# Weight blocks split once and kept in DRAM, with the three token groups written out

## The reference

```
p = rms_norm(x, norm_g) @ w_in
aq, ak, av, ag, bq, bfg, bi, bg, ma, mb = split_projection(p)
...
ya = (attn_o * silu(ag)) @ w_ba
rn = rec_o * rsqrt(mean(rec_o * rec_o) + EPS) * g_norm
yb = (rn * silu(bg)) @ w_bb
merged = sigmoid(ma) * ya + sigmoid(mb) * yb
y = rms_norm(x + merged @ w_o, final_norm_gain)
```

## Time and profile before

| what | value |
|---|---|
| median of 3 runs | 1633.92 us (1633.89 to 1634.69) |
| the profiled execution's own time | 1631.52 us |
| its span in the profile | 1629.7 us |
| mean granted TensorE clock | 0.992 of full |
| PE busy | 1571.6 us, 96% |
| DVE busy | 896.3 us, 55% |
| ACT busy | 578.5 us, 35% |
| POOL busy | 437.2 us, 27% |
| moved by DMA | 124.35 MB, mean 76 GB/s |
| POOL L441, `w_lo` | 174 times, 423.0 us |
| ACT L473, `w_hi` | 174 times, 182.8 us |

### The profile page before, as it was taken

How to read it: one execution, slowest core, us unless ns; L and a number is a source line. 1 busy time by engine, 2 the same in 40 slices (tenths; PEclk the granted TensorE clock), 3 DMA queues, 4 the chain that set the end, 5 groups by cost and what they waited for, 6 DMA issues and landing times.

```text
span 1629.7 us, 24842 instructions
## 1 busy us (share of the span) xinstructions
PE 1571.6 (96%) x9679; PEld 1467.7 (90%) x9679; DVE 896.3 (55%) x1302; ACT 578.5 (35%) x1118; POOL 437.2 (27%) x186
## 2 busy tenths in 40 slices
PE   7999999999999899999999999999999999999997
PEld 5989899999997698989999999779898999999975
DVE  5667987721237356878782222745687868222213
ACT  5355443322123334555332212342455533222212
POOL 1321122332323232212223322423222222333320
PEclk9999999999999999999999999999999999999999
DMA  4211111122243321111112223433111111221231
GB/s 170 86 58 43 43 56 43 52 81 76 65 169 103 129 85 52 43 43 52 43 56 84 72 65 112 160 115 110 53 43 40 56 43 56 78 78 66 65 136 71
DMA packets 44856, 124.35 MB, mean 76 GB/s; under 512 B 6209, under 2 KB 17217, under 8 KB 44737
## 3 DMA queue, kind: packets, MB, share of 16 engines
q1 hardware_dynamic: 39408, 120.35, 23.2%
q10 hardware_dynamic: 5328, 2.37, 0.5%
HBM read 111.69 MB, written 11.01 MB: 75 GB/s over the span
## 4 chain that ended last, share of the span: by engine, by line
PE 87%; DVE 9%; issue 2%; ACT 1%; DMA 0%; DVEq 0%; ACTq 0%
PE bank L984 22%; PE bank L986 22%; PE bank L985 22%; PE bank L1185 4%; PE bank L1186 4%; PE bank L1187 4%; DVE rs L936 2%; PE bank L1156 1%; PE bank L1082 1%; PE bank L1138 1%; PE bank L1100 1%; PE bank L1114 1%; PE bank L1152 1%; PE bank L1124 1%; PE bank L1091 1%
## 5 line engine op out<-in xcount | busy, mean ns | idle before, releaser
L441 POOL TENSOR_TENSOR w_lo<-w_raw,w_hi 128x1024 fp32r<-128x1024 f32 x174 | 423.0, 2433 | 1152.5 <-ACT w_hi L473 1152.5
L984 PE MATMUL bank<-x_hi,w_hi 128*128 128x320 f32 (+1 forms) x2016 | 660.9, 328 | 10.1 <-issue 6.2
L986 PE MATMUL bank<-x_hi,w_lo 128*128 128x320 f32 (+1 forms) x2016 | 651.5, 323 | 0.0
L985 PE MATMUL bank<-x_lo,w_hi 128*128 128x320 f32 (+1 forms) x2016 | 651.1, 323 | 0.0
L984 PEld LDWEIGHTS bank<-x_hi,w_hi 128*128 128x128 f32 x2016 | 380.6, 189 | 19.0 <-issue 9.0
L985 PEld LDWEIGHTS bank<-x_lo,w_hi 128*128 128x128 f32 x2016 | 380.9, 189 | 0.1
L986 PEld LDWEIGHTS bank<-x_hi,w_lo 128*128 128x128 f32 x2016 | 380.3, 189 | 0.0
L473 ACT ACTIVATE w_hi<-w_raw 128x1024 fp32r<-128x1024 f32 x174 | 182.8, 1054 | 163.8 <-DMA w_raw<-in_w 157.2
L946 DVE TENSOR_TENSOR sig_a<-sig_a,bank 128x320 f32<-128x320 f32 (+1 forms) x48 | 25.0, 522 | 344.3 <-PE bank L986 344.3
L1185 PE MATMUL bank<-w_hi,m_hi 128*128 128x512 f32 (+1 forms) x288 | 116.2, 404 | 3.9 <-issue 3.7
L1187 PE MATMUL bank<-w_hi,m_lo 128*128 128x512 f32 (+1 forms) x288 | 113.9, 395 | 0.0
(11 more groups left out here) (169 smaller groups left out, 2034.8 us busy)
## 6 DMA issues: line engine op xcount, KB each, us to landing
w_raw<-in_w SPq DMA_DIRECT2D x174, 512.0 KB, 3.6
res<-in_x SPq DMA_DIRECT2D x15, 512.0 KB, 7.5
out_y<-res SPq DMA_DIRECT2D x15, 512.0 KB, 3.8
x_raw<-in_x_t SPq DMA_DIRECT2D x12, 384.0 KB, 7.1
x_raw<-in_x_t SPq DMA_DIRECT2D x12, 320.0 KB, 4.6
cos<-in_rope_cos SPq DMA_DIRECT2D x3, 352.0 KB, 3.8
sin<-in_rope_sin SPq DMA_DIRECT2D x3, 352.0 KB, 5.0
out_state_first<-s_first ACTq DMA_DIRECT2D x12, 64.0 KB, 3.3
```

Of the source, the lines that this page charges most:

```text
L441: pool.tensor_tensor(w_lo[s][:], w_raw[s][:], w_hi[s][:].bitcast(F32), ALU.subtract).then_inc(w_split, 1)
L984: pe.matmul(out, w_h, m_h, start=first, stop=False)
L985: pe.matmul(out, w_h, m_l, start=False, stop=False)
L986: return pe.matmul(out, w_l, m_h, start=False, stop=last_of_bank)
```

## The change

The weights are split only while the first group is worked on. High and low part of a slot are now one tile `w_both`; once a block is split, SP writes both parts (1 MB) to a DRAM tensor `w_parts`. In the later groups SP loads both parts from there straight into the slot, and TensorE waits for the load itself. ACT and POOL split nothing in these groups. In the first group the load of the next block into a slot also waits until the slot's parts are written (`w_kept`). The loop is gone: the three bodies stand in the program one behind the other.

```
     for s in range(SLOTS):
-        w_hi.append(own(f"w_hi{s}", [P, KT, P], F32R))
-        t, at, _ = sb(f"w_lo{s}", [P, KT, P], F32R)
-        w_lo.append(t)
-        w_raw.append(own(f"w_raw{s}", [P, KT, P], F32, at))
+        t, at, end = sb(f"w_both{s}", [P, 2, KT, P], F32R)
+        w_both.append(t)
+        w_hi.append(t[:, 0])
+        w_lo.append(t[:, 1])
+        w_raw.append(own(f"w_raw{s}", [P, KT, P], F32, (at + end) // 2))
+
+    parts = nc.dram_tensor("w_parts", (NB, P, 2, KT, P), F32).ap()
...
     def groups(eng, body):
 
-        with eng.Fori(0, GROUPS - 1) as g:
-            body(g, False)
-        body(GROUPS - 1, True)
+        for g in range(GROUPS):
+            body(g, g == GROUPS - 1)
...
                     wait_full(sp, gg, last, s, bank_of(last, s))
-            sp.dma_start(w_raw[SLOT[b]][:], w[b]).then_inc(w_landed[SLOT[b]], 16)
+                if gg == 0:
+                    sp.wait_ge(w_kept[SLOT[b]], 16 * (nth_in_slot(c) + 1))
+            if g == 0:
+                sp.dma_start(w_raw[SLOT[b]][:], w[b]).then_inc(w_landed[SLOT[b]], 16)
+            else:
+                sp.dma_start(w_both[SLOT[b]][:].bitcast(F32), parts[b]).then_inc(w_landed[SLOT[b]], 16)
+
+        def keep_block(b):
+
+            sp.wait_ge(w_split, b + 1)
+            sp.dma_start(parts[b], w_both[SLOT[b]][:].bitcast(F32)).then_inc(w_kept[SLOT[b]], 16)
...
+            kept = 0
             for b in range(SLOTS, NB):
+                while g == 0 and kept <= before(b)[0]:
+                    keep_block(kept)
+                    kept += 1
                 load_block(g, b, True, last)
...
+            if g == 0:
+                for b in range(kept, NB):
+                    keep_block(b)
             if not last:
                 for b in range(SLOTS):
                     load_block(g + 1, b, True)
...
             for b in range(FIRST, NB):
-                low(g, b)
+                if g == 0:
+                    low(g, b)
                 if b == NB - 5 and not last:
                     add_squares(pool, 1, g + 1)
-            if not last:
-                for b in range(FIRST):
-                    low(g + 1, b)
...
                 b = BLOCK[n] + 2
-                if b < NB:
-                    if b >= FIRST:
-                        high(g, b)
-                elif not last:
-                    high(g + 1, b - NB)
+                if g == 0 and FIRST <= b < NB:
+                    high(g, b)
...
+        def wait_block(g, b):
+
+            if g == 0:
+                pe.wait_ge(w_split, b + 1)
+            else:
+                pe.wait_ge(w_landed[SLOT[b]], 16 * (PER_SLOT[SLOT[b]] * g + nth_in_slot(b) + 1))
```

More of the change, by code:

```diff
@@ L205, in program @@
     res = own("res", [P, NT, D_MODEL], F32, at_ga_hi)
-    w_hi, w_lo, w_raw = [], [], []
+    w_both, w_hi, w_lo, w_raw = [], [], [], []
     for s in range(SLOTS):
-        w_hi.append(own(f"w_hi{s}", [P, KT, P], F32R))
-        t, at, _ = sb(f"w_lo{s}", [P, KT, P], F32R)
-        w_lo.append(t)
-        w_raw.append(own(f"w_raw{s}", [P, KT, P], F32, at))
+        t, at, end = sb(f"w_both{s}", [P, 2, KT, P], F32R)
[4 more added lines that the diff above has]
+    parts = nc.dram_tensor("w_parts", (NB, P, 2, KT, P), F32).ap()
     fgain = own("fgain", [P, D_MODEL])
@@ L272, in program @@
     w_high, w_split = sem("w_high"), sem("w_split")
+    w_kept = [sem(f"w_kept{s}") for s in range(SLOTS)]
     piece_used = sem("piece_used")
@@ L667, in body @@
                     ahead(f"wo{a}{s}")
-                    if (a, s) == (1, 3) and not last:
-                        high(g + 1, 2)
                 elif kind.startswith("x_"):
@@ L1021, in body @@
                     if s == 0:
-                        pe.wait_ge(w_split, NB * g + b + 1)
+                        wait_block(g, b)
                     wait_bank_free(pe, g, last, step, bank)
```

## The result

The changed kernel takes 1605.95 us (1605.1 to 1608.06, 4 runs) against 1634.31 us (1633.89 to 1635.53): a ratio of 0.9825, 95% interval 0.9811 to 0.984. It is 28.4 us faster; 21.7 had been forecast, and the time lies just under the range of 1606 to 1621. The profiled execution took 1606.46 us and its span is 1604.6 us. What follows is about the 6.7 us that the forecast lacked as much as about the 21.7.

What follows compares the result with a forecast made beforehand. PE's matmuls were taken to bound the kernel, leaving only its waits and low clock to win. Terms 6.9 + 9.8 + 4.1 + 0.5 + 0.4 = 21.7 us gave 1609.8 profiled, 1612.2 as median; range 1606 to 1621.

Steps and rivals of the forecast that it cites:

- gap at the first boundary: Loop's branch after group one: PE's stand falls from 5.71 to 0.49 us, 5.2 us won.
- clock behind it: PE's half-clock stretch after the 5.7 us issue wait at the loop's branch goes: 1.7 us won.
- `sc_t` waits: PE's waits for `sc_t` shrink in groups two and three as DVE's `sarg` and `f` run unstretched: 3.3 and 3.1 us.
- clock behind `sc_t` and `q_rot`: Half-clock stretches go: 2 x 1.7 us behind two `sc_t` waits, 1.7 behind the third group's `q_rot` wait.
- `q_rot` waits: `swap` in the chain drops from 2.1 to 0.89 us: 1.2 us of each wait in two groups, 2.4 us.
- `attn_o`: Third group's 0.54 us PE wait, put down to timing shifted behind a clock drop, goes: 0.5 us.
- state update and `sq_lo`: PE's `sq_lo` waits in two groups: 0.2 us won each, 0.4 in all; the read-out wait was not priced.
- issue gaps inside the groups: Small PE issue waits ahead of the output projections: given no term in the forecast, so 0 us.
- stores in group one: 58 stores of 1.05 MB on SP's queue: load and store take 6.1 to 6.6 us against 7.4 available; price zero.
- only the loop counts: Rival, chance 0.08: another engine takes over PE's waits at `sc_t` and `q_rot`; 6.9 us are left, 1627 us.
- PE is early and waits later: Rival, chance 0.08: PE reaches read-outs and `sq_lo` about 4 us earlier, giving half of 14.8 us back: 1619.6 us.
- The slower case: Rival, chance 0.06: stores hold loads back in group one, 9.2 us per block, 26 us of PE waits, 1638 us.

Runs made afterwards that it cites:

- ma0: Changed kernel, but one block, the 27th subtraction of a group, is loaded raw and split by ACT and POOL in every group: 1609.47 us.
- the loop alone: Kernel before with only the loop written out, every group still split by ACT and POOL: 1627.19 us against 1633.88, ratio 0.9958.
- the second store: Changed kernel, but each first-group block is stored twice, to two DRAM tensors, and the next load waits for both: 1669.7 us.

## Why the prediction was right and where it fell short

The terms of the sum, with what the two traces show for the second and third group and the boundaries:

| term | forecast | measured |
|---|---|---|
| gap at the first boundary | 5.2 | 5.4 (5.71 to 0.35) |
| clock behind it | 1.7 | 1.7 |
| `sc_t` waits | 6.4 | 7.0 (3.62 and 3.37, both to 0) |
| clock behind `sc_t` and `q_rot` | 5.1 | 5.1 (three drops) |
| `q_rot` waits | 2.4 | 2.7 (2.37 and 2.17 to 0.94 each) |
| `attn_o` | 0.5 | 0.5 (0.54 to 0) |
| state update and `sq_lo` | 0.4 | 4.1 (0.79 + 1.45 + 0.53 + 1.31, all to 0) |
| issue gaps inside the groups | 0 | 2.0 (3.7 to 1.9, and 0.49 to 0.26 at the second boundary) |
| stores in group one | 0 | 0 |
| sum | 21.7 | 28.5 |

The medians differ by 28.4. The profiled spans differ by 25.1 only; in the changed kernel's profiled execution the clock fell in the first group behind `q_rot` too and stayed low for 6.8 us behind `sc_t`, twice 1.7 us more than in that of before. That the sum meets the difference of the medians to 0.1 us is in part luck: the profiled execution of before lay 2.8 us under its median, that of the changed kernel 0.5 us over it.

**The mechanism was right.** The loop's branch, the stretched DVE operations and the clock behind the waits are where the time came from, each within 0.6 us, and the stores were free. In the long stretch of the first group a store landed in 6.5 us, which with the 0.4 us between the issues makes 6.9 us for load and store, where the prediction had 6.1 to 6.6; the loads are 7.4 us apart, so half a microsecond was to spare and not one. The Trainium skill ("DMA: Bandwidth & Descriptors", section "Measured (HBM→SBUF, 128 partitions, SWDGE, issued from GpSimd)") has 6.15 us for 1 MB. Here, on SP's queue, a load of 1 MB from `w_parts` took 4.8 us at its median from issue to landing, and a second store behind the first adds only 2 us. So the measurements decide against the sum of 9.2 us for load and store.

**The step that failed is the `sq_lo` term.** The prediction read the 0.23 us ahead of the operation at 818.28 as "waited only 0.23 us for DVE's own state update; beyond that it is bound to PE's projection". The timeline of DVE in the kernel before shows the opposite:

```profile
808.62 0.56 DVE L827 TENSOR_TENSOR raw<-bank,raw 128x384 f32<-128x384 f32 x1 [1.30 <-ACT raw L577]
809.21 0.56 DVE L832 TENSOR_TENSOR raw<-raw,attn_o 128x384 f32<-128x384 f32 x1
809.80 2.45 DVE L751 CAST ga_hi<-raw 128x384 fp32r<-128x384 f32 x1
...
814.08 3.59 DVE L907 SCALAR_TENSOR_TENSOR st<-st,decay,bank 128x128 f32<-128x128 f32 x9
817.71 0.35 DVE L907 SCALAR_TENSOR_TENSOR carry_s<-st,decay,bank 128x128 f32<-128x128 f32 x1
```

and that of ACT, when the input of the operation at 818.28 was made:

```profile
813.34 0.44 ACT L577 ACTIVATE raw<-bank 128x320 f32<-128x320 f32 x1 [3.81 <-PE bank L986]
```

From 808.62 on DVE works without a pause worth the name until the reciprocal of `finish`; that input had been ready since 813.8. A short idle time ahead of an operation whose releaser is its own engine means that the engine is the chain, not that the wait is short of a cause. The cast at 809.80 takes 2.45 us instead of 0.36, and everything behind it is 2.1 us late. The experiment with `ma0` shows it: this one subtraction brings both waits back, 3.5 us in two groups. So the term was 4.1 us and not 0.4: 2.8 for `sq_lo`, 1.3 for the wait ahead of the read-outs, which the prediction did not price at all. Some 0.4 of the 4.1 are the loop's, as the experiment on the loop alone shows.

**A second part was put at nothing:** the issue gaps ahead of the output projections, 2.0 us. They were in the waits as small entries, and the loop alone takes them from 3.7 to 1.9 us. The program of before has a register instruction ahead of each of these waits, which the unrolled one has not; that this is the cause is argued, not shown. What speaks for it is the third group, outside of the loop in both: its four gaps are 0.23 to 0.26 us in either kernel. Without these two parts even the upper bounds of the prediction's terms, 6.9, 10.4, 6.3, 0.5 and 2.8, make 26.9 us, less than the 28.4 measured.

**The rivals.** That only the loop counts is refuted: the loop alone gives 6.7 us of the 28.4. That PE is early and waits later did not happen: the chain ahead of the reciprocals had 2 us of POOL in it as well. The slower case is real but was priced too low: the second store makes the 9.2 us per block that it assumed, and that costs 64 us and not 26. Where between 7.4 and 9.2 us it begins was not measured.

## What to carry to other kernels

Work that an engine does off the critical path can still set the time through the engine that it holds up: compare the longest with the shortest duration of one line, and when the long ones end together with another engine's operation, ask which of them lie in a chain that is waited for. Only their place counts: of subtractions of 2.4 to 3.1 us in the later groups, two cost 3.5 us, four others 10 us and another six nothing. Cutting such an operation into pieces can be worth more than its own overhead, here 9.5 us for 81 us more of POOL's time, half of it by the clock drops that went with the waits.

## What the runs showed of the hardware

- A DVE operation on 128x4 numbers took 2.3 us beside a POOL subtraction with both inputs in SBUF, and 0.16 us without it. Casts and copies with one input were stretched as well (`ga_hi` 2.45 instead of 0.36). The reciprocal was not: it took 4.54 us with a whole subtraction beside it, as without.
- The loop's branch cost TensorE 5.0 to 5.4 us at the one place where it was taken (5.71 and 5.34 us in two profiles, 0.35 without it). Inside the loop each of TensorE's waits for DVE was 0.14 to 0.26 us longer than in the same program written out.
- Behind one and the same wait of 3.4 us the clock fell for 3.4 us in one place, for 6.8 in another, and in one case not at all; behind 2.2 us it fell in some executions. Each 3.4 us at half clock are 1.7 us of the time. The seven runs of the kernel before on one chip lie 5.3 us apart, with a mean clock of 0.992 in the shortest and 0.988 in the two longest.
- A store of 1 MB behind a load of 512 KB landed in 6.5 us, and the second of two stores behind it in 8.5. A load of 1 MB landed in 4.8 us.
- ACT waits in its program's order: where its rounding stood for a late load (7.37 us), the copy behind it was late too, and TensorE waited 2.49 us for that.
